# A two-layer encoder on one core: three column sums moved, the roundings of unit 0 on another engine, and 16 products at the start

## The reference

```python
for l in range(2):
    x = x + hybrid_mixer(rms_norm(x, norm_mix_g[l]), w_in[l], ...)
    x = x + mem_cross_attention(rms_norm(x, norm_xattn_g[l]), mem, ...)
    x = x + conv_ffn(rms_norm(x, norm_ffn_g[l]), w_up[l], ...)
return rms_norm(x, norm_final_g)

def hybrid_mixer(h, ...):
    pa, pq, pk, pv, pc, pg = split(h @ w_in)
    ya = silu(layer_norm(causal_dwconv(pa[:, :512] * sigmoid(pa[:, 512:]), conv_w, conv_b)))   # 31 taps
    yb = differential attention of pq, pk, pv with a relative bias
    yc = u * (w_s * causal @ layer_norm(v) + b_s)        # u, v = gelu(pc); w_s: 4 groups of 128 x 128
    merged = sum of sigmoid(pg_i + gate_b_i) * (y_i @ w_br[i])
    return merged @ w_out
```

## Time and profile before

| | us |
|---|---|
| median of three runs | 1896.15 (1895.87 to 1898.44) |
| the profiled execution | 1895.55 |
| its span in the profile | 1893.8 |
| TensorE busy in the span | 1810.9 (96%) |
| VectorE busy | 1245.0 (66%) |
| ScalarE busy | 728.2 (38%) |
| GpSimd busy | 457.3 (24%) |

### The profile page before, as it was taken

One profiled execution on the slowest core, in us unless ns is written; L12 is line 12 of the kernel. 1 busy time (PEld: TensorE's weight loads), 2 busy tenths in 40 slices (PEclk: granted clock), 3 DMA queues, 4 the chain that ended last, 5 costly groups with the idle time before them and its releaser, 6 DMA issues. The chain is left out here.

```text
span 1893.8 us, 22363 instructions
## 1 busy us (share of the span) xinstructions
PE 1810.9 (96%) x8572; PEld 1499.3 (79%) x8572; DVE 1245.0 (66%) x1629; ACT 728.2 (38%) x943; POOL 457.3 (24%) x166
## 2 busy tenths in 40 slices
PE   7699899999989999999999999999999899999996
PEld 5598778887967878888888887788888687888885
DVE  4697665556447875775779765565644587775594
ACT  4132354534434443333343234444443543332341
POOL 1244000100202324434224410001030132434430
PEclk8899899999999999999999998999999999999998
DMA  5232122232311332322332321223233123322321
GB/s 221 92 128 95 67 73 99 85 134 90 128 51 67 112 111 89 111 89 89 111 134 89 123 79 69 99 89 115 86 112 111 45 89 111 111 90 89 112 89 45
DMA packets 28327, 186.08 MB, mean 98 GB/s; under 512 B 3480, under 2 KB 3608, under 8 KB 7740
## 3 DMA queue, kind: packets, MB, share of 16 engines
q1 hardware_dynamic: 26332, 172.64, 25.3%
q0 software_dynamic: 1648, 11.54, 1.6%
q10 hardware_dynamic: 240, 0.48, 0.1%
HBM read 179.33 MB, written 7.68 MB: 99 GB/s over the span
## 5 line engine op out<-in xcount | busy, mean ns | idle before, releaser
L1311 PE MATMUL ps<-x_hd,w_hd 128*128 128x512 f32 x1600 | 629.1, 393 | 20.7 <-DVE v_sb L875 15.4
L1312 PE MATMUL ps<-x_tl,w_hd 128*128 128x512 f32 x1600 | 625.3, 391 | 0.0
L472 POOL TENSOR_TENSOR w_tl<-raw,w_hd 128x2048 fp32r<-128x2048 f32 x78 | 361.1, 4629 | 541.9 <-ACT w_hd L595 405.7
L595 ACT ACTIVATE w_hd<-raw 128x2048 fp32r<-128x2048 f32 (+1 forms) x157 | 299.3, 1906 | 332.5 <-PE ps L1312 274.8
L1321 PE MATMUL ps<-x_hd,w_tl 128*128 128x512 f32 x1600 | 383.9, 391 | 0.0
L1311 PEld LDWEIGHTS ps<-x_hd,w_hd 128*128 128x128 f32 x1600 | 302.0, 189 | 92.8 <-issue 22.5
L1321 PEld LDWEIGHTS ps<-x_hd,w_tl 128*128 128x128 f32 x1600 | 301.8, 189 | 62.8
L1312 PEld LDWEIGHTS ps<-x_tl,w_hd 128*128 128x128 f32 x1600 | 302.0, 189 | 62.3 <-issue 0.2
L791 DVE TENSOR_TENSOR w_tl<-raw,w_hd 128x2048 fp32r<-128x2048 f32 x78 | 178.8, 2292 | 130.3 <-ACT w_hd L595 83.2
L1311 PE MATMUL ps<-ring_hd,w_hd 128*128 128x512 f32 (+1 forms) x672 | 257.0, 386 | 3.8 <-DVE resid L1071 3.5
L1312 PE MATMUL ps<-ring_tl,w_hd 128*128 128x512 f32 (+1 forms) x672 | 254.1, 382 | 0.0
(11 more groups left out here) (155 smaller groups left out, 1556.4 us busy)
## 6 DMA issues: line engine op xcount, KB each, us to landing
raw<-units SPq DMA_DIRECT2D x155, 1024.0 KB, 4.8
resid<-x_t SPq DMA_DIRECT2D x4, 512.0 KB, 8.6
bias_t<-bias_tiles POOLq DMA_DIRECT2D x8, 256.0 KB, 4.5
cg<-mem_t POOLq DMA_DIRECT2D x2, 1024.0 KB, 5.2
resid<-x_t POOLq DMA_DIRECT2D x1, 2048.0 KB, 8.7
resid_dram<-resid POOLq DMA_DIRECT2D x1, 2048.0 KB, 8.4
resid<-resid_dram POOLq DMA_DIRECT2D x1, 2048.0 KB, 9.1
out<-resid SPq DMA_DIRECT2D x4, 512.0 KB, 2.7
```

Source lines behind the costliest of these rows:

```text
L472: line.done(pool.tensor_tensor(w_tl[:, k % 2, :], raw[:, k % 2, :], w_hd[:, k % 2, :].bitcast(F32), ALU.subtract), of_unit("tail", g))
L595: line.done(act.activation(out, in_, func, **kw), *labels)
L1311: pe.matmul(dst, w_hd[:, slot, w], hd[:, src, :], start=kc == 0, stop=False)
L1312: i = pe.matmul(dst, w_hd[:, slot, w], tl[:, src, :], start=False, stop=False)
```

## The change

- `spatial_sums` goes to banks 6 and 7 and stands right behind unit 0; it waits also until the bias strip is copied out of these banks. Unit 2 no longer waits for `bs1_3`.
- `spatial_biases` on VectorE goes from behind step 1 to ahead of `mean_square("n0")`. GpSimd masks w_s ahead of `power("n0")`.
- In layer 0 the column sums of `n0` go to the middle of unit 1 and wait for `bs1_3`, and the spread goes behind unit 1. Layer 1 keeps them in unit 0 (`NORM_AT = (1, 0)`).
- VectorE, no longer ScalarE, rounds the two halves of unit 0. The tails of units 0 and 1 come ahead of VectorE's sums of squares. ScalarE makes the head of unit 1 ahead of the squares. A small activation stands ahead of ScalarE's first wait.
- `column_sums("c")` goes from behind unit 14 into the middle of the first product of unit 15, in both layers. On VectorE `last_sum("c")` and `mean_square("c")` go to the end of step 14, behind `attention_last`.
- TensorE starts with 16 products of `ones` with itself into bank 5.

```diff
-                power("n0", rs0, ms, 4)
                 if l == 0:
                     pool.wait_ge(ws_in, 16 * 2)
...
+                power("n0", rs0, ms, 4)
+                if l:
...
+            op(junk[:, 0:4], half_neg[:], ACT.Identity, needs=("half_neg",))
             act.wait_ge(pvec_in, 16)
...
+            for t in range(KD):
+                act.wait_ge(x_in[t // 2], 16)
+                first_head(0, t)
+            head_of_unit(1)
             for t in range(KD):
                 first_square(0, "n0", t)
-                if t == 3:
-                    head_of_unit(1)
...
                 first_tail(0, t)
+                if t == 1:
+                    dve.wait_ge(half_in, 16)
+                    op(lambda: dve.tensor_copy(w_hd[:, 0, 0:half], raw[:, 0, 0:half]), "half_head", independent=1)
                 if t == 3:
+                    dve.wait_ge(weights_in[0], 16)
+                    op(lambda: dve.tensor_copy(w_hd[:, 0, half:UNIT], raw[:, 0, half:UNIT]), of_unit("head", 0),
+                       independent=1)
+                if t == 5:
...
+            tail_of_unit(0)
+            dve.wait_ge(weights_in[1], 16)
+            tail_of_unit(1)
             for t in range(KD):
                 first_sum(0, "n0", t)
...
-                    dve.wait_ge(weights_in[1], 16)
-                    tail_of_unit(1)
+                    spatial_biases()
                 mean_square("n0", ms, 4, D)
...
-                    if k == CLN + 1:
-                        last_sum("c", KB)
...
-                    if k == CLN + 1:
-                        mean_square("c", ms, 4, BR)
...
                     attention_last(k)
+                    if k == CLN + 1:
+                        last_sum("c", KB)
+                        mean_square("c", ms, 4, BR)
...
             pe.wait_ge(gpsimd_done, line.at("ones"))
+            for _ in range(16):
+                pe.matmul(ps[:, 5, 0:P], ones[:], ones[:], start=True, stop=True)
...
             def spatial_sums():
+                pe.wait_ge(vector_done, line.at("strip_copied"))
                 for lay in range(DEPTH):
                     pe.wait_ge(gpsimd_done, line.at(f"ws_mask{lay}"))
-                    line.done(pe.matmul(ps[:, 4 + lay, :], ones[:], v_sb[:, lay, :], start=True, stop=True), f"wsum{lay}")
+                    line.done(pe.matmul(ps[:, 6 + lay, :], ones[:], v_sb[:, lay, :], start=True, stop=True), f"wsum{lay}")
...
-                elif e in FIRST_ON and FIRST_ON[e] == 2:
-                    pe.wait_ge(vector_done, line.at(f"bs{DEPTH - 1}_3"))
...
+            def first_sums():
+                column_sums("n0", (f"bs{DEPTH - 1}_3",) if l == 0 else ())
+
+            def conv_sums():
+                column_sums("c", ("c_cent3",))
...
+                        sums = (first_sums if k == NORM_AT[l] else (lambda: column_sums("r2")) if k == 44
+                                else first_scores if k == 41 else
+                                conv_sums if k == CLN + 2 and e == FIRST_OF[k] else None)
...
-                    if k == CLN + 1:
-                        column_sums("c", ("c_cent3",))
```

More of the change, by code:

```diff
@@ L161 @@
 assert NU % 2 == 0
+NORM_AT = (1, 0)
 BY_ACT = {"w", "v", "xk", "xv"}
@@ L384, in build @@
             UNIT_KINDS.setdefault(u, []).append((e, kind, arg))
+        FIRST_OF = {u: es[0][0] for u, es in UNIT_KINDS.items()}
         LAST_OF = {u: [e for e, kind, _ in es if kind != "sv"][-1] for u, es in UNIT_KINDS.items()}
@@ L481, in _ @@
             line.begin(0)
-            line.done(pool.memset(half_neg[:], -0.5))
+            line.done(pool.memset(half_neg[:], -0.5), "half_neg")
             line.done(pool.memset(ones[:], 1.0), "ones")
@@ L834, in _ @@
             dve.wait_ge(pvec_in, 16)
+            half = UNIT // 2
             for t in range(KD):
@@ L874, in spatial_biases @@
                         c = _cols["gln_b"] + g
-                        op(lambda: dve.scalar_tensor_tensor(dst, ps[:, 4 + lay, P * g:P * g + P], pv_all[:, lay, c:c + 1],
+                        op(lambda: dve.scalar_tensor_tensor(dst, ps[:, 6 + lay, P * g:P * g + P], pv_all[:, lay, c:c + 1],
                                                             dst, ALU.mult, ALU.add), f"bs{lay}_{g}",
@@ L1179, in _ @@
                     if l == 0:
-                        if k == 1:
-                            spatial_biases()
                         if k == 2:
@@ L1307, in product @@
                     if unit == 0 and kc == nk // 2:
-                        pe.wait_ge(scalar_done, line.at(of_unit("head", 0)))
+                        pe.wait_ge(vector_done, line.at(of_unit("head", 0)))
                     for t in tiles:
@@ L1424, in _ @@
                     g = l * NU + k
-                    pe.wait_ge(scalar_done, line.at(of_unit("head", g) if g else "half_head"))
+                    if g:
+                        pe.wait_ge(scalar_done, line.at(of_unit("head", g)))
+                    else:
+                        pe.wait_ge(vector_done, line.at("half_head"))
                     for e, kind, arg in UNIT_KINDS[k]:
-                        sums = ((lambda: column_sums("n0")) if k == 0 else (lambda: column_sums("r2")) if k == 44
-                                else first_scores if k == 41 else None)
+                        sums = (first_sums if k == NORM_AT[l] else (lambda: column_sums("r2")) if k == 44
+                                else first_scores if k == 41 else
+                                conv_sums if k == CLN + 2 and e == FIRST_OF[k] else None)
                         i = spatial(e, arg) if kind == "sv" else product(e, kind, arg, g, sums)
                         line.done(i, f"e{e}", *((of_unit("over", g),) if e == LAST_OF[k] else ()))
-                    if k == 0:
+                    if g == 0:
+                        spatial_sums()
+                    if k == NORM_AT[l]:
                         if l == 0:
@@ L1435, in _ @@
                         spread("n0", 4, rs0)
-                        if l == 0:
-                            spatial_sums()
                     if k == CLN:
```

5 lines of the change are left out of this document (removed).

## The result

The changed kernel takes 1884.80 us (median of 4 runs, 1884.64 to 1885.28) where the kernel before took 1896.01 (4 runs, 1895.27 to 1898.44): 11.2 us less. The ratio is 0.9939, with a 95% interval of 0.9922 to 0.9956, so it is faster, by 0.6%. The forecast was 1880.3, with a range of 1875 to 1888. The profiled execution has a span of 1883.5 us, 10.3 under that of before.

A forecast was written before the change was run, and what follows sets the result against it. TensorE, working 96% of the span, was taken as the bound. 26.4 us gained in the opening less 10.6 lost at the conv norms made 15.8 us gained, hence 1880.3 us, with a range of 1875 to 1888.

The forecast's parts named there:

- Term A: Opening up to unit 2: an earlier start at 38.05 and full clock gain 26.4 us.
- The masks: GpSimd's masks in the opening: could push VectorE back 1.22 us at most; costed at nothing, 1 us in the range.
- The clock at the start: Units 0 and 1: half clock there would cost 2 to 3 us; costed at nothing, 2 us in the range.
- ScalarE's head of unit 5: Behind lambda's exponential: ready at 68.9, unit 5 starting at 70.7; costed at nothing, 2 us in the range.
- rivals 2 and 3: 2 (0.08): half of Term A lost behind GpSimd's tails, 1890.3; 3 (0.04): VectorE bounds units 3 to 13, kernel slower.
- Term B: Conv norm in each layer: TensorE waits 11.4 us for VectorE's last sum, then half clock; 5.3 us lost each, 10.6 together.
- Rival 1: Conv norm: sums are ready when TensorE comes, saving 9.0 us in each layer, 1851.8; chance 0.06.

The follow-up runs named there:

- e7: The changed kernel run and profiled again, unaltered: 1884.23 us.
- e4: The changed kernel with VectorE's last conv sum and mean put back to their old places, TensorE's column sums kept inside unit 15: 1860.29 us.
- e3: The kernel before with one call moved: VectorE adds the spatial biases at the end of step 0, ahead of unit 1's taps: 1879.30 us.
- e9: e4 with VectorE taking the scores' maxima ahead of the tail in the four steps with scores B: 1852.14 us.

## Why the prediction was right, and where it was short

The direction, both mechanisms and their places hold, and the measured time lies in the range, 4.5 us from the forecast. Of the 15.8 us forecast 11.2 came.

- **Term A, 26.4:** measured 26.67. VectorE decides the start as said: the tail of unit 0 was ready at 19.5 (19.8 forecast), TensorE waited 0.95 (1.4), the biases ended at 31.41 (31.3), unit 2 started at 37.63 (38.05). Two errors under 1 us cancel. A rounding takes 0.69, not the 1.15 that I took, and most of it fell in a wait; and VectorE's two tails took 4.93 in place of 4.58. How close 26.4 came is partly luck: it was read from a profile whose start was 1.6 us longer than that of the second, and against the second the same opening gains 25.1.
- **The masks:** GpSimd was the one held up, and VectorE by only 0.2 us in its second tail (2.51 in place of 2.29). The masks took 3.94 us instead of 1.22, from 18.65 to 22.59, while VectorE's tails ran from 17.16 to 22.09. They were still in time for the spatial sums at 23.28, so they cost nothing, as put in.
- **The clock at the start and ScalarE's head of unit 5:** nothing lost. TensorE waited for no evacuation of VectorE up to unit 13, so rivals 2 and 3 fall.
- **Term B, twice 5.3:** measured 6.05 and 5.01 in the first profile, 5.26 and 5.01 in e7. The wait was 11.25, 11.4 forecast, and the spread stood 29.4 us behind the end of unit 14 (28 forecast). What moved is the stretch at half clock: in layer 0 the 32 products behind the column sums lost 2.8 us, and 2.0 in e7, where I had 2.0.
- **Rival 1** falls, since the wait was there. e4 shows that its mechanism was right for the place, 9.06 and 9.35 us a layer against its 9.0, had VectorE's last sum been left where it was. Its time of 1851.8 was not reached even so (1860.29), since the next wait came up.
- **The missing part** is a term that the sum did not have. By the first profile of before, 5.4 us in the first profile of the changed kernel and 4.4 in e7 went nearly all in products at half clock behind small waits that the change does not touch; by the second profile of before it is some 3.4. I had read the clock at the two places of the change and nowhere else, and took the one profile of before as the rule for all other waits.
- **The range** was added up wrongly: 26.4 less the 3 and the 2 us named for term A is 21.4, not 23. With it the worst end is 1887.8, still inside the 1888 given.

## What to carry to other kernels

An instruction that others wait for belongs where its inputs are ready, and its place is read from the order of the engine that runs it, not from that of the engine that asks for it: a sum put at the end of its step made TensorE wait 11 us in each layer, where it could have waited for nothing (e4), and eight bias additions put ahead of twelve taps gave 16 us (e3). A wait removed shows the next one at once (e4 against e9), so price that wait too. Behind a wait TensorE may also run at half clock. In these profiles that cost from nothing to 2.8 us a time and differed between executions of one kernel, so compare several profiles before giving 2 us a cause. Two equal spans can hide differences that cancel.

## What the hardware showed beside this

- GpSimd was slowed beside VectorE as VectorE is beside GpSimd: two masks took 3.94 us beside VectorE's tails (1.22 alone), and each ended 0.5 us behind a tail, at 19.96 and 22.60 where the tails ended at 19.46 and 22.10.
- VectorE rounds 128 x 1024 from SBUF to SBUF in 0.69 us, ScalarE in 1.06 in the trace of before. A subtraction of 128 x 2048 takes VectorE 2.29, so per element a rounding costs 0.6 of it.
- The same 1.73 us wait was followed by none, seven or eight products at half clock, in two executions of one kernel even by none and seven.
